# Slots by parity, a first pair in quarters and a loop over the middle pairs in a mixture-of-experts kernel

## What is computed

```
h2      = rms_norm(h, norm2_g)
group   = argmax(h2 @ w_group)                 # 8 groups of 8 experts
e1, e2  = top 2 experts of that group by h2 @ w_router
y[t]    = sum over e in (e1, e2): weight[t, e] * (silu(h2[t] @ w1[e]) * (h2[t] @ w3[e])) @ w2[e]
out     = h + y
```

## Time and profile before

| | |
|---|---|
| median of 3 runs | 1592.67 us (1592.53 to 1593.77) |
| the profiled execution's own time | 1589.25 us |
| its span, first to last instruction | 1587.5 us |
| TensorE, VectorE, ScalarE busy | 77%, 27%, 14% of the span |
| read from HBM | 499.78 MB |
| the slowest wait on the chain that ended last | DMA into arena, 37% of the span |

### The profile page before, as it was taken

One profiled execution on the slowest core, in us unless ns is written; L12 is line 12 of the kernel. 1 busy time (PEld: TensorE's weight loads), 2 busy tenths in 40 slices (PEclk: granted clock), 3 DMA queues, 4 the chain that ended last, 5 costly groups with the idle time before them and its releaser, 6 DMA issues.

```text
span 1587.5 us, 16162 instructions
## 1 busy us (share of the span) xinstructions
PE 1226.7 (77%) x6741; PEld 655.9 (41%) x6741; DVE 432.2 (27%) x1021; ACT 218.9 (14%) x527; POOL 18.2 (1%) x30
## 2 busy tenths in 40 slices
PE   8999999999999999996556557556556566467467
PEld 4665788854488644542212212222122122122122
DVE  3344333383154666331110110111111111111101
ACT  3334323211022101210000000000000000000000
POOL 2000000000000000100000000000000000000000
PEclk9999999999999999998878878878778778778779
DMA  9441177413542356799999999999999999999997
GB/s 297 159 160 54 55 275 248 147 52 134 183 159 86 127 211 273 300 422 427 428 427 427 428 429 426 428 428 428 428 427 427 428 428 427 428 428 427 428 427 322
DMA packets 91378, 501.80 MB, mean 316 GB/s; under 512 B 6653, under 2 KB 34673, under 8 KB 65456
## 3 DMA queue, kind: packets, MB, share of 16 engines
q1 hardware_dynamic: 90544, 500.00, 77.6%
q0 software_dynamic: 768, 0.85, 0.4%
HBM read 499.78 MB, written 1.05 MB: 315 GB/s over the span
## 4 chain that ended last, share of the span: by engine, by line
PE 58%; DMA 38%; DVE 3%; ACT 1%; issue 1%; SPq 0%; ACTq 0%; DVEq 0%
DMA arena<-in_w 37%; PE ps L1358 9%; PE ps L1039 8%; PE ps L719 7%; PE ps L1234 6%; PE ps L714 5%; PE ps L1380 4%; PE ps L1091 3%; PE ps L1341 2%; PE ps L1389 2%; PE ps L898 2%; PE ps L1286 2%; PE ps L1054 1%; DVE moe_turned L2249 1%; PE ps L1369 1%
## 5 line engine op out<-in xcount | busy, mean ns | idle before, releaser
L1358 PE MATMUL ps<-arena,hT 128*32 128x512 f32 x2048 | 284.9, 718 | 319.1 <-DMA arena<-in_w 316.0
L1358 PEld LDWEIGHTS ps<-arena,hT 128*32 128x32 f32 x2048 | 79.2, 129 | 523.6 <-issue 523.6
L2247 DVE TENSOR_TENSOR moe_hid<-moe_hid,ps 64x512 f32<-64x512 f32 x32 | 22.1, 690 | 547.6 <-ACT moe_hid L2596 547.6
L1039 PE MATMUL ps<-hT,arena 128*128 128x256 f32 x640 | 138.3, 379 | 0.0
L1380 PE MATMUL ps<-arena,moe_turned 128*32 128x512 f32 x1024 | 116.7, 595 | 25.2 <-DVE moe_turned L2249 25.1
L1039 PEld LDWEIGHTS ps<-hT,arena 128*128 128x128 f32 x640 | 121.5, 190 | 16.5
L2596 ACT ACTIVATE moe_hid<-ps 64x512 f32<-64x512 f32 x32 | 18.8, 588 | 737.7 <-PE ps L1358 737.7
L719 PE MATMUL ps<-hT,arena 128*128 128x256 f32 x512 | 113.9, 380 | 0.1
L719 PEld LDWEIGHTS ps<-hT,arena 128*128 128x128 f32 x512 | 96.8, 190 | 15.0 <-issue 2.2
L714 PE MATMUL ps<-arena,hT 128*128 128x512 f32 x192 | 84.1, 594 | 0.0
L1234 PE MATMUL ps<-arena 128*128 128x512 f32 x176 | 77.0, 592 | 0.0
(11 more groups left out here) (408 smaller groups left out, 1108.0 us busy)
## 6 DMA issues: line engine op xcount, KB each, us to landing
arena<-in_w SPq DMA_DIRECT2D x191, 2048.0 KB, 38.9
arena<-in_w_in SPq DMA_DIRECT2D x18, 2048.0 KB, 8.2
arena<-in_w_up SPq DMA_DIRECT2D x22, 1024.0 KB, 7.2
arena<-in_w_down SPq DMA_DIRECT2D x5, 2048.0 KB, 12.2
arena<-in_w_out SPq DMA_DIRECT2D x2, 2048.0 KB, 14.3
arena<-in_w_conv_out SPq DMA_DIRECT2D x2, 2048.0 KB, 7.9
arena<-in_w_attn_out SPq DMA_DIRECT2D x2, 2048.0 KB, 7.8
arena<-in_w_o SPq DMA_DIRECT2D x2, 2048.0 KB, 8.0
```

What stands on the lines that cost most here:

```text
L1039: last = mm(ps[:, 2 * s + a, g * S:(g + 1) * S], up[:, c, g, a * P:(a + 1) * P], hT[:, c, :], start=(c == 0), stop=(c == KC - 1))
L1358: last = mm(ps[k * CAP:(k + 1) * CAP, UP, :], x[:, c, (k % 2) * CAP:(k % 2 + 1) * CAP], w[:, at:at + DE], start=(c == 0), stop=(c == KC - 1))
```

## The change

- **Slots.** Pairs use fixed slots by parity: pair 0 slots 0 to 5; odd pairs (6, 7, 8, 0, 9, 10); the other even pairs (1, 2, 3, 0, 4, 5). So slot 0 is in every pair, as its fourth load. `moe_count` gives the semaphore value for a slot's n-th content, as some contents now come in several DMAs.
- **Order of issue.** Pairs 1 and 2 load in the order k = 0, 1, 2, 4, 5, 3. After pair 1's first load, and with no wait of their own, the upper half of slot 9 and the lower half of slot 10 are loaded; the other halves follow when wo1 has been used (slot 9) and when the residual's last product is done (slot 10, semaphore `res_taken`). `h_res` is moved to the upper half of arena 3.
- **Pair 0** comes in quarters (two chunks of the 1024 rows for both experts and both matrices, `load_quarter`), and its up product (`first_up`) goes chunk by chunk, with `quarter_used` after chunks 0, 1, 3 and 5. Slot 0's next content is loaded in halves after chunks 0 and 1, slot 1's after chunk 3, slot 2's after chunk 5, slot 3's at the end.
- **Gather.** One pair at a time: 8 chunks of 64 columns (`gather_pair`), one `xg`, one `sel`, one `moe_turned` for all pairs; ScalarE takes 8 pieces of 64 columns (`take_pair`); VectorE chooses for two experts in each pair.
- **Loop.** TensorE's pairs 1 to 30 are a loop of 15 turns over two pairs, with waits against a value worked out from the turn. The other engines stay unrolled.

```diff
-            for unit in range(PAIRS * UNITS_PAIR):
-                moe_wait(unit)
...
+            for pair in range(PAIRS):
+                for k in (0, 1, 2, 4, 5, 3) if pair in (1, 2) else range(UNITS_PAIR):
+                    if (pair, k) == (1, 1):
+                        load_part(4, 1)
+                        load_part(5, 0)
+                    if pair == 1 and k in (4, 5):
+                        moe_wait(pair, k)
+                        load_part(k, k - 4)
+                        continue
+                    if (pair, k) == (1, 3):
+                        sp.wait_ge(quarter_used, 1)
+                        sp.dma_start(MOE_SLOTS[0][:, 0:2048], t["w3"][3, :, 0:2048]).then_inc(moe_loaded[0], 16)
+                        moe_wait(1, 3)
+                        sp.dma_start(MOE_SLOTS[0][:, 2048:4096], t["w3"][3, :, 2048:4096]).then_inc(moe_loaded[0], 16)
+                        continue
+                    moe_wait(pair, k)
...
+            def moe_wait(pair, k):
+                at = moe_slot(pair, k)
+                if moe_turn(pair, k) > 1:
...
+                    if prior == 0 and j < 3:
+                        sp.wait_ge(quarter_used, (2, 3, 4)[j])
+                    elif prior in HALVED:
+                        sp.wait_ge((up_half, up_half, up_filled, up_filled, down_half, y_filled)[j], prior + 1)
+                    else:
+                        sp.wait_ge((up_filled, up_filled, up_filled, up_filled, y_filled, y_filled)[j], prior + 1)
...
+                elif at == NSLOT - 1:
+                    sp.wait_ge(rms_ready, 8)
+                    sp.wait_ge(h_moved, 4)
+                    sp.wait_ge(res_taken, 1)
...
+            def gather_pair():
+                for c in range(KC):
+                    for half in range(2):
+                        last = mm(ps[:, GT, c * 2 * CAP:(c + 1) * 2 * CAP], hview[:, half, c, :], sel[:, half, :],
+                                  start=(half == 0), stop=(half == 1))
+                last.then_inc(gathered, 1)
...
+            def first_up():
+                for c in range(KC):
+                    if c % 2 == 0:
+                        wait_unit(0, c // 2)
+                    w = MOE_SLOTS[c // 2]
+                    for k in range(4):
+                        at = ((c % 2) * 4 + k if c < 2 else k * 2 + c % 2) * DE
+                        last = mm(ps[k * CAP:(k + 1) * CAP, UP, :], xg[:, c, (k % 2) * CAP:(k % 2 + 1) * CAP],
+                                  w[:, at:at + DE], start=(c == 0), stop=(c == KC - 1))
+                    if c in (0, 1, 3, 5):
+                        last.then_inc(quarter_used, 1)
+                last.then_inc(up_filled, 1)
...
+            def pair_turn(p, i):
+                units = [MOE_SLOTS[moe_slot(p, k)] for k in range(UNITS_PAIR)]
+                def loaded(k):
+                    step = moe_turn(p + 2, k) - moe_turn(p, k)
+                    pe.wait_ge(moe_loaded[moe_slot(p, k)], i * (16 * step) + moe_count(moe_slot(p, k), moe_turn(p, k)))
+                for k in range(4):
+                    loaded(k)
+                pe.wait_ge(hid_ready, i * 2 + p)
+                pe.wait_ge(xg_ready, i * 2 + (p + 2))
+                expert_up(xg, units, False, 0, up_half)
+                expert_up(xg, units, False, 1, up_filled)
+                pe.wait_ge(y_ready, i * 2 + p)
+                scatter(selwT, scattered)
+                pe.wait_ge(sel_ready, i * 2 + (p + 3))
+                gather_pair()
...
+            pair_step(0)
+            with nc.tensor.Fori(0, len(LOOPED) // 2) as i:
+                pair_turn(1, i)
+                pair_turn(2, i)
+            pair_step(PAIRS - 1)
```

More of the change, by code:

```diff
@@ L367, in two_blocks, with moe_slot, moe_turn, moe_count @@
         NSLOT = len(MOE_SLOTS)
+        SLOTS_EVEN, SLOTS_ODD = (1, 2, 3, 0, 4, 5), (6, 7, 8, 0, 9, 10)
+        def moe_slot(p, k):
+            return ((SLOTS_EVEN if p else (0, 1, 2, 3, 4, 5)), SLOTS_ODD)[p % 2][k]
+        def moe_turn(p, k):
+            at = moe_slot(p, k)
+            return sum(moe_slot(q, j) == at for q in range(p + 1) for j in range(UNITS_PAIR))
         HALVED = (0, PAIRS - 1)
-        xg = [hT[:, :, b * P:(b + 1) * P] for b in range(2)]
-        sel = [sel_first, router_w[:].rearrange("p c n -> p (c n)")[:, 0:2 * P].rearrange("p (a s) -> p a s", a=2)]
+        LOOPED = range(1, PAIRS - 1)
+        def moe_count(slot, turn):
+            return 16 * turn + ((48 if turn == 1 else 64) if slot == 0 else 16 if slot in (1, 2, 3, 9, 10) else 0)
+        xg = hT[:, :, 0:2 * CAP]
         kept = carve(route)
@@ L610, in _ @@
+                    load.then_inc(moe_loaded[moe_slot(pair, k)], 16)
             sp.wait_ge(slots_ready, 1)
@@ L1412, in _ @@
             mm(ps[:, 6, NE:2 * NE], ones, assign[:, 1, :], start=False, stop=True).then_inc(ranks_ready, 1)
-            mm(ps[:, 1, :], ident, h_res[:, 0, 512:1024], start=True, stop=False, skip_group_check=True)
+            mm(ps[:, 1, :], ident, h_res[:, 0, 512:1024], start=True, stop=False, skip_group_check=True).then_inc(res_taken, 1)
             pe.wait_ge(sel_ready, 2)
             pe.wait_ge(h_moved, 4)
[L1416 to L1419, removed]
-                halved = p in HALVED
[L1421 to L1428, removed]
+            gather_first(1)
@@ L2178, in _, with choose, experts @@
             iota = const("slot_iota")
-            def choose(e0, n, buf, done, halves=(0, 1)):
+            def choose(e0, done, halves=(0, 1)):
                 for half in halves:
-                    for k in range(n):
-                        last = v.tensor_scalar(sel[buf][:, half, k * CAP:(k + 1) * CAP], iota, slot[:, half, e0(k)],
+                    for k in range(2):
+                        last = v.tensor_scalar(sel[:, half, k * CAP:(k + 1) * CAP], iota, slot[:, half, e0(k)],
                                                rstd[:, half:half + 1], ALU.is_equal, ALU.mult)
                 last.then_inc(done, 1)
-            def quad(q):
-                return lambda k: slice(4 * q + k, 4 * q + k + 1)
+            def experts(p):
+                return lambda k: slice(2 * p + k, 2 * p + k + 1)
             def weigh(e0, done):
```

181 lines of the change are left out of this document (96 added, 85 removed).

## The result

The changed kernel took 1583.21 us in the median of four runs (1583.06 to 1586.18), the kernel before 1593.22 in four: ratio 0.9937, interval 0.9922 to 0.9952, ten microseconds less. Timed twice more with more runs beside it, it gave 0.9955 (0.9941 to 0.9970) and 0.9957 (0.9943 to 0.9972), about 7 us. Forecast were 5.5 us and 1587.2, with 1583.7 as the low end, so the first measurement lies just outside the range. The sign was right; the sizes have to be looked at term by term.

The account below looks back on a forecast made before the run. The experts' stage was taken to be bound by its DMA stream at 428 GB/s. Gains of 3.7 + 1.8 = 5.5 us took the profiled 1589.25 to 1583.75; 3.42 more for the median gave 1587.2, range 1583.7 to 1592.2.

Parts of the forecast that it names:

- Steps 1 and 2: Start of the experts' stage: half-free slots and earlier refills cut the dry stream; gain 3.7 us, bounds 2.5 to 4.7.
- Steps 3, 4 and 7: Pair 0 in quarters, gather per pair, and the tail: no cost or change.
- rival B: Pairs 0 and 1: longer gather delays refills of slots 4 and 0; gain 3.3 us or less; chance 0.15.
- Step 5: Looped pairs, slot 0 used by every pair: queue has 10 us or more to spare, so cost nothing.
- Step 6: TensorE's loop over pairs 1 to 30: about 27 code packets at 0.065 us each, gain 1.8 us (nothing to 4.3).
- The sum against the median: Whole kernel: 5.5 us off the profiled 1589.25 gives 1583.75; the median, 3.42 above the profile, gives 1587.2.
- A: TensorE's loop body is fetched anew, 45 to 60 packets in fifteen turns: gain 2.1 us, 1590.6; chance 0.17.
- C: Gate on slot 0 in the loop: the load queue runs out each pair; 9.5 us slower, 1602.2; chance 0.08.
- D: Start of the experts' stage: early refills do nothing, only the loop gains, 1590.9; chance 0.03.

Follow-up runs that it names:

- loops on three engines: The changed kernel with VectorE's and ScalarE's pairs in loops too, besides TensorE's: 1584.79 us, ratio 0.9949; run again 1582.75 us, 0.9938.
- body of six pairs: The changed kernel with TensorE's loop body over six pairs (five turns) instead of two: 1590.29 us, ratio 0.9982 to the kernel before.
- body of ten pairs: The changed kernel with TensorE's loop body over ten pairs (three turns) instead of two: 1593.18 us, ratio 0.9994 to the kernel before.

## Why the prediction was right and wrong

The forecast was 1587.2, the first measurement 1583.2, 4.0 us lower. By the profiles 0.7 of them are the sum's (6.2 for 5.5), and 3.3 are those of the distance from the profile to the median (0.15 for 3.42). The steps in turn:

**Steps 1 and 2 (start): right.** Forecast 3.7 us with bounds of 2.5 to 4.7; measured 3.5 and 0.3 more at P0, which is within what P0 moves by itself. The missing stream was put at 6.2 us and is 6.5. Issues expected at 677.2, 681.0 and 683.7 came at 677.15, 680.93 and 683.51. What I said less well is where the gain lies: I counted the first hole as the thing that is filled, but the runs show that what counts is the restart after chunk 0, and that the halves pay because of the chunks.

**Steps 3, 4 and 7: nothing, or nearly.** Pair 0's down product was put at 696.3 and pair 1's up product at 699.9; the latter started at 699.30 and the stretch from 700 to 712 moved 433 GB/s, so rival B did not come. The tail, "no change", is 0.3 us longer, and 1.8 in the profile in which the clock fell in it.

**Step 5 (slots by parity): right for the kernel as it is, not shown beyond that.** The stream stays at 428 GB/s with the shorter queue, the up product waits for DMA in each pair, and with loops on three engines all double periods are down at 58.72 to 58.75. But written out the new kernel has a steady part 2.0 us longer than that of the kernel before, and four more packets account for 0.6 of it. So with much code in the stream the new arrangement doesn't seem free, which the forecast put at nothing; the cause is open.

**Step 6 (the loop): the mechanism right, the term mis-sized.** I priced a code packet at its share of the engines' time, 0.065 us, and 27 of them at 1.8. The steady part fell by 2.7 us, 0.10 for each of these 27, and against the same kernel written out the loop gains 4.8, 0.15 a packet. The step that failed is "1.04 us of one engine, so 0.065 us of the whole stream". My reading is that a product waits for the whole of a load, each part of which one of the 16 engines moves, so that the work of one engine can delay a load by more than a sixteenth; no run looked at a single engine. The upper bound (4.3 in the text; its own difference gives 4.4) was not the better price for this change, which got 2.7 of it. It is what the kernel with loops on three engines reaches: 767.73 - 763.5 = 4.2. The argument from the first block's loop against a window of two blocks was weaker than I made it: a body of 17 KB can lie in two blocks of 16 KB, so that a loop without fetches fits both figures. The body of six pairs tells them apart.

**The sum against the median: the step that failed most.** "The median of the runs shown is 3.42 above it" was taken as a fixed distance. It isn't one. The kernel before has its median 4.0 us above the first profiled execution (1593.22 against 1589.25) and 0.1 above the second (1595.55 against 1595.45); the changed kernel has 0.15, 0.05 and 0.6. The two profiles of the kernel before differ by 4.9 us at P0, which is the granted clock before 150 us. The first had no stretch at half clock there, so it was a lucky profile to start from, while the first four runs of the changed kernel, of 1583.06 to 1586.18, came out lower than its later ones. Over three timings the ratios give a gain of 7 to 10 us, and the two later ones, 7.2 and 6.8, are nearest to what the profiles say. What lies between the first ten microseconds and the profiles' 6.2 is thus draw, as far as is known: no trace of the other runs exists.

**Rivals.** A (the body doesn't stay) is what the body of ten pairs does, at 0.9994; with two pairs it didn't happen. C did not come: two pairs take 58.75 us. D falls with the 3.5 us at the start.

## What to carry to other kernels

In a stage that is bound by a stream of DMAs, fetched code is part of the traffic and costs more than its bytes: a body that the engine can keep (here one of some 120 KB on TensorE) is worth a loop even where the engine itself has time to spare. At the start of such a stage, ask when the stream can run on without a stop; a hole that is filled ahead of another release is worth only what that release leaves. And compare kernels by parts of one profile between two events of the program, since the times carry the clock's draw from other stages.

## What was not expected of the hardware

- TensorE's granted clock is at half speed for some microseconds before 150 us in some executions and not in others of the same kernel; 0.58 from 105 to 110 us in one, 1.00 in another. With one such stretch P0 is 1.4 us later (3.4 us at half clock) to 3.4 us later (6.8 us). In five of the fourteen profiles another one falls into the last down product, which then takes about 5.3 us for 4.0.
- A single packet of 8 KB of other engines' code went with a pair that was 0.9 us longer (30.13 for 29.20), and with the packet gone so was the 0.9; others cost nothing.
- TensorE kept a loop of some 120 KB (estimated) without a fetch between its first turn and its end, and refetched one of some 200 KB in each turn (37 packets in three turns).
- 160 waits that are already met take TensorE 6.3 us.
- A loop on ScalarE with Silu and Copy in its body loads the activation table in each turn (1.28 us); written out it did not.
